# Decay masks by predicated copy, y summed by an accumulating store, the state's share of y scaled in PSUM

## The reference, cut to what matters

```python
acs = jnp.cumsum(dt * a, axis=2)                       # per chunk and head
seg = acs[:, :, :, None] - acs[:, :, None, :]
decay = jnp.exp(jnp.where(lower, seg, -jnp.inf))
cb = jnp.einsum('bctgn,bcsgn->bctsg', cc, bc)
y_diag = jnp.einsum('bctsgr,bcsgrp->bctgrp', cb[..., None] * decay, xdt)
y_off = jnp.einsum('bctgn,bcgrpn,bctgr->bctgrp', cc, s_in, jnp.exp(acs))
...
y_f, s_f = ssd_chunked(xs, dt[:, :, 0], a[0], bm, cm, h0_f)
y_b, s_b = ssd_chunked(rev(xs), rev(dt[:, :, 1]), a[1], rev(bm), rev(cm), h0_b)
y = y_f + rev(y_b) + d_skip[:, None] * xs
```

## Time and profile before

| | |
|---|---|
| runs, us | 2822.95, 2816.64, 2823.3 |
| profiled execution, us | 2829.5 |
| its span, us | 2827.7 |
| mean granted TensorE clock | 0.976 |
| TensorE matmul busy | 2672.9 us (95% of the span) |
| VectorE busy | 1658.7 us (59%) |
| ScalarE busy | 608.1 us (22%) |
| GpSimd busy | 988.0 us (35%) |

### The profile page before, as it was taken

How to read it: one execution, slowest core, us unless ns; L and a number is a source line. 1 busy time by engine, 2 the same in 40 slices (tenths; PEclk the granted TensorE clock), 3 DMA queues, 4 the chain that set the end, 5 groups by cost and what they waited for, 6 DMA issues and landing times. The chain is left out here.

```text
span 2827.7 us, 32173 instructions
## 1 busy us (share of the span) xinstructions
PE 2672.9 (95%) x12390; PEld 2146.4 (76%) x12390; DVE 1658.7 (59%) x2219; ACT 608.1 (22%) x871; POOL 988.0 (35%) x515
## 2 busy tenths in 40 slices
PE   8889999999999999987888999989989999999997
PEld 5778777778888888866775776578767888888885
DVE  6887555756556665676747986953475222222247
ACT  4222242311110011133232104632131110001111
POOL 2122225554333343541212432012645333333353
PEclk9999999999999999998999999999989999999998
DMA  3111132223222332221001343241322111111122
GB/s 139 39 51 45 51 142 82 97 82 98 97 89 91 102 96 96 97 101 61 31 30 38 112 127 112 99 177 45 116 93 90 53 45 47 50 52 45 52 69 102
DMA packets 88484, 228.88 MB, mean 81 GB/s; under 512 B 27520, under 2 KB 30720, under 8 KB 88384
## 3 DMA queue, kind: packets, MB, share of 16 engines
q1 hardware_dynamic: 52384, 172.81, 18.3%
q10 hardware_dynamic: 36000, 54.69, 6.1%
HBM read 197.98 MB, written 28.31 MB: 80 GB/s over the span
## 5 line engine op out<-in xcount | busy, mean ns | idle before, releaser
L215 POOL CAST w_hi<-w_raw 128x1024 fp32r<-128x1024 f32 x254 | 289.0, 1138 | 1774.6 <-PE ps L228 1755.8
L224 PE MATMUL ps<-a_hi,w_hi 128*128 128x512 f32 x2080 | 694.7, 402 | 47.3 <-PEq L2942 14.5
L217 POOL TENSOR_TENSOR w_lo<-w_raw,w_hi 128x1024 fp32r<-128x1024 f32 x254 | 696.0, 2740 | 20.3
L226 PE MATMUL ps<-a_lo,w_hi 128*128 128x512 f32 x2080 | 677.9, 393 | 0.0
L228 PE MATMUL ps<-a_hi,w_lo 128*128 128x512 f32 x2080 | 676.7, 393 | 0.0
L224 PEld LDWEIGHTS ps<-a_hi,w_hi 128*128 128x128 f32 x2080 | 391.4, 191 | 151.0 <-issue 58.3
L226 PEld LDWEIGHTS ps<-a_lo,w_hi 128*128 128x128 f32 x2080 | 396.1, 190 | 83.3
L228 PEld LDWEIGHTS ps<-a_hi,w_lo 128*128 128x128 f32 x2080 | 395.3, 190 | 84.3
L226 PE MATMUL ps<-g_b,w_hi 128*128 128x512 f32 x1216 | 412.6, 391 | 0.0
L224 PE MATMUL ps<-g_b,w_hi 128*128 128x512 f32 x1088 | 364.4, 392 | 11.2 <-DVE g_b L1806 11.2
L228 PE MATMUL ps<-g_b,w_lo 128*128 128x512 f32 x1088 | 362.1, 390 | 0.0
(11 more groups left out here) (459 smaller groups left out, 2682.2 us busy)
## 6 DMA issues: line engine op xcount, KB each, us to landing
w_raw<-in_wstream SPq DMA_DIRECT2D x254, 512.0 KB, 3.5
ada_w<-in_ada_w ACTq DMA_DIRECT2D x25, 512.0 KB, 3.5
ada_w_b<-in_ada_w ACTq DMA_DIRECT2D x25, 512.0 KB, 3.5
y_by_token<-y ACTq DMA_DIRECT2D x12, 512.0 KB, 3.3
x_res_b<-in_xT SPq DMA_DIRECT2D x2, 2048.0 KB, 11.2
x_block<-x_res_b SPq DMA_DIRECT2D x16, 256.0 KB, 3.0
z_rows<-ada_w ACTq DMA_DIRECT2D x8, 512.0 KB, 2.9
u_rows<-pad ACTq DMA_DIRECT2D x8, 512.0 KB, 4.2
```

The source lines that it names most:

```text
L215: pool.tensor_copy(k.w_hi[:, s, :], k.w_raw[:, s, :]).then_inc(k.w_high, 1)
L217: pool.tensor_tensor(k.w_lo[:, s, :], k.w_raw[:, s, :], k.w_hi[:, s, :].bitcast(F32), ALU.subtract).then_inc(k.w_split, 1)
L224: pe.matmul(o, w_hi, a_hi[:, c], start=first, stop=False)
L226: pe.matmul(o, w_hi, a_lo[:, c], start=False, stop=False)
```

## The change

Four things are changed, all in the scan.

1. The masks. `exponents(i, g)` is now called once for each group and writes both directions unmasked, 4 matmuls over 64 rows each: the first direction in `pair[0]`, the second in `pair[1]`. VectorE then copies the second over the first where a mask is not zero (`choose`, a predicated copy within PSUM), and ScalarE takes one exponential for each group. The 2 sums `add_decays` go. The identity matmuls and `scan_square` go.
2. The diagonal of the second direction, which the choice leaves out, is a weight for each token and head, `own`; it is computed in phase4 (products of B and C on VectorE, their sums by 16 matmuls with one column, `own_sums`) and takes the place of `d_skip` in L2656.
3. The state's share of y is scaled in place in PSUM, and the diagonal products (`own_chunk`) add onto it (`start=False`). ScalarE copies the sum out (`copy_out`).
4. y is not loaded back. GpSimd issues a store to `y_tok` that adds (`accum_op`).

The orders change with it. The diff, with declarations, sizes of waits and the loads of `stage` left out:

```diff
 # phase4, VectorE, after the fourth convolution
+            dve.wait_ge(s["silu"], 2 * XS0)
+            for g in range(NGRP):
+                for c0, c1, home in own_bc[g]:
+                    tt(home, v.bc[:, g, c0 * P:c1 * P], v.bc[:, NGRP + g, c0 * P:c1 * P], ALU.mult).then_inc(s["own_in"], 1)
 # phase4, TensorE, before the wait for sums_ready
+            for g in range(NGRP):
+                for c0, c1, home in own_bc[g]:
+                    for c in range(c0, c1):
+                        ins = pe.matmul(own_sums[:, g * NC + c:g * NC + c + 1], home[:, (c - c0) * P:(c - c0 + 1) * P],
+                                        k.mean_col[:, :], start=True, stop=True)
 # phase5, GpSimd
+            for i in range(NC):
+                pool.wait_ge(s["y_ready"], NC + i + 1)
+                pool.dma_start(d.y_tok[i, :, :], y_of[i % 2], accum_op=ALU.add).then_inc(y_out[i % 2], 16)
+            for q in range(2):
+                pool.wait_ge(y_out[q], 16 * NC // 2)
 # phase5, TensorE
+            def exponents(i, g):
                 pe.wait_ge(s["moving_ready"], i + 1)
+                if i or g:
+                    pe.wait_ge(s["e_ready"], NGRP * i + g)
+                if i and g == 0:
+                    pe.wait_ge(s["cb_ready"], i)
+                for b in range(2):
+                    at = g * HPG + b * HPG // 2
+                    for r in range(2):
+                        rows = slice(r * P // 2, (r + 1) * P // 2)
+                        ins = pe.matmul(k.ps[:, 2 * r + b, :].rearrange("p (h t) -> p h t", t=P), v.l_rows[rows, here(i)],
+                                        moving[rows, at:at + HPG // 2, :], start=True, stop=True)
             def products_cb(i):
-                pe.wait_ge(s["e_ready"], EXPS * i + 3)
+                pe.wait_ge(s["chosen"], NGRP * (i + 1))
+            def own_chunk(i, g):
+                pe.wait_ge(s["w_ready"], NGRP * i + g + 1)
+                for h in range(g * HPG, (g + 1) * HPG):
+                    ins = pe.matmul(..., start=False, stop=True)
             def forward(i):
                 ...
                 ins.then_inc(s["off_done"], 1)
+                if i + 1 < NC:
+                    exponents(i + 1, 0)
                 pe.wait_ge(s["xw_ready"], back + NC + i + 1)
                 if i:
                     pe.wait_ge(s["y_ready"], NC + i)
                 ...
                 ins.then_inc(s["st_done"], 1)
                 if i + 1 < NC:
-                    exponents(i + 1)
+                    exponents(i + 1, 1)
+                pe.wait_ge(s["fore_ready"], i + 1)
+                own_chunk(i, 0)
+                if i + 1 < NC:
                     products_cb(i + 1)
+                own_chunk(i, 1).then_inc(s["diag_done"], 1)
 # phase5, ScalarE
             def exps(i):
+                if i >= 2:
+                    act.wait_ge(s["diag_done"], i - 1)
+                for g in range(NGRP):
+                    act.wait_ge(s["chosen"], NGRP * i + g + 1)
+                    act.activation(big[:, i % 2 * NGRP + g, :], pair[0], ACT.Exp).then_inc(s["e_ready"], 1)
+            def copy_out(i):
+                act.wait_ge(s["diag_done"], i + 1)
+                if i >= 2:
+                    act.wait_ge(y_out[i % 2], 16 * (i // 2))
+                ...
+                act.activation(y_of[i % 2], Xf[(i + 1) % 2], ACT.Copy).then_inc(s["y_ready"], 1)
                 if i + 1 < NC:
                     exps(i + 1)
                     copy_cb(i + 1)
-                    if i + 2 < NC:
-                        make_moving(i + 2)
+                copy_out(i)
+                if i + 2 < NC:
+                    make_moving(i + 2)
                 if i < SPLIT_EARLY:
                     act.wait_ge(s["d_in"], 16 * (i + 1))
                     act.activation(v.a_hi[:, i, :], stage[:, :], ACT.Copy).then_inc(s["dhi"], 1)
-                act.wait_ge(s["y_ready"], NC + i + 1)
-                act.dma_start(d.y_tok[i, :, :], y_of[i % 2]).then_inc(y_out[i % 2], 16)
 # phase5, VectorE
+            def choose(i, g):
+                dve.wait_ge(s["d_done"], NGRP * i + g + 1)
+                fore, rear = (p.rearrange("p (h t) -> p h t", h=HPG) for p in pair)
+                dve.copy_predicated(fore, bc(after, 1, HPG), rear).then_inc(s["chosen"], 1)
             for i in range(NC):
-                add_decays(i)
-                if i:
-                    last_sum(i - 1)
                 dve.wait_ge(s["cb_ready"], i + 1)
                 for g in range(NGRP):
+                    dve.wait_ge(s["e_ready"], NGRP * i + g + 1)
+                    decays = big[:, i % 2 * NGRP + g, :].rearrange("p (h t) -> p h t", h=HPG)
+                    tt(decays, decays, bc(cb[:, g, :], 1, HPG), ALU.mult).then_inc(s["w_ready"], 1)
+                if i:
+                    low_part(i - 1)
                 dve.wait_ge(s["off_done"], i + 1)
+                y = heads(Xf[(i + 1) % 2])
+                tt(y, y, per_head(v.e_acs, i, 0), ALU.mult).then_inc(s["fore_ready"], 1)
+                if i + 1 < NC:
+                    choose(i + 1, 0)
                 dve.wait_ge(s["state_ready"], i + 1)
                 ch.link(tt(heads(state[:, :]), heads(state[:, :]), per_head(v.e_tot, i, 0), ALU.mult))
+                if i + 1 < NC:
+                    choose(i + 1, 1)
+                dve.wait_ge(s["st_done"], i + 1)
                 tt(state[:, :], state[:, :], Xf[i % 2], ALU.add).then_inc(s["state_ready"], 1)
                 if i + 1 < NC:
                     weigh(i + 1, 0)
```

More of the change, by code:

```diff
@@ L10 @@
 F32R = mybir.dt.float32r
+I32 = mybir.dt.int32
 ACT = mybir.ActivationFunctionType
@@ L1951, in open_scan @@
     v.rows = sb("head_rows", [P, 80])
+    v.own = sb("own_weight", [P, NC, SSM_HEADS])
     return v
@@ L2322, in _ @@
             dve.wait_ge(s["scan_in"], 16)
-            dve.tensor_copy(v.square[:, 0, :], k.mats[:, IDENT, :]).then_inc(s["chain"], 1)
-            dve.tensor_copy(v.square[:, 1:3, :], v.consts[:, 0:2 * P].rearrange("p (r t) -> p r t", r=2)).then_inc(s["chain"], 1)
+            dve.wait_ge(s["own_out"], 1)
+            for g in range(NGRP):
+                hs = slice(g * HPG, (g + 1) * HPG)
+                rear = slice(SSM_HEADS + g * HPG, SSM_HEADS + (g + 1) * HPG)
+                ch.link(tt(v.own[:, :, hs], dt[:, 0:NC, rear], bc(own_sums[:, g * NC:(g + 1) * NC], 2, HPG), ALU.mult))
+            ch.link(stt(out=v.own[:, :, :], in0=v.own[:, :, :], scalar=1.0 * D_MODEL,
+                        in1=bc(v.rows[:, 64:64 + SSM_HEADS], 1, NC), op0=ALU.mult, op1=ALU.add))
             dve.wait_ge(s["sums_rows"], 1)
@@ L2376, in phase5 @@
         BWD_JOBS = 2
-        EXPS = 2 * NGRP
-        ident_r, masks = v.square[:, 0, :], [v.square[:, 1 + r, :] for r in range(2)]
+        after = v.consts[:, SC_FORE:SC_FORE + P].bitcast(I32)
         back = 2 * CC
@@ L2453, in here @@
                 return slice(i * P, (i + 1) * P)
-            def exponents(i):
+            def exponents(i, g):
                 pe.wait_ge(s["moving_ready"], i + 1)
-                for j in range(EXPS):
-                    g, r, use = j // 2, j % 2, EXPS * i + j
-                    if use >= 2:
-                        pe.wait_ge(s["e_ready"], use - 1)
-                    if i and j == 0:
-                        pe.wait_ge(s["cb_ready"], i)
-                    rows = slice(r * P // 2, (r + 1) * P // 2)
-                    outs = [k.ps[:, 2 * r + b, :].rearrange("p (h t) -> p h t", t=P) for b in range(2)]
-                    for out in outs:
-                        pe.matmul(out, ident_r, bc(masks[r], 1, HPG // 2), start=True, stop=False)
-                    for b, out in enumerate(outs):
-                        at = g * HPG + b * HPG // 2
-                        ins = pe.matmul(out, v.l_rows[rows, here(i)], moving[rows, at:at + HPG // 2, :], start=False, stop=True)
-                    ins.then_inc(s["d_done"], 1)
+                if i or g:
[8 more added lines that the diff above has]
+                                        moving[rows, at:at + HPG // 2, :], start=True, stop=True)
+                ins.then_inc(s["d_done"], 1)
@@ L2492, in forward @@
                 if i + 1 < NC:
[L2493 removed]
+                    exponents(i + 1, 1)
+                pe.wait_ge(s["fore_ready"], i + 1)
+                own_chunk(i, 0)
+                if i + 1 < NC:
                     products_cb(i + 1)
[L2495 to L2502 removed]
+                own_chunk(i, 1).then_inc(s["diag_done"], 1)
             for q in range(2):
                 pe.wait_ge(k.pair_free[q], UZ_END // 2)
[L2506 removed]
+            for g in range(NGRP):
+                exponents(0, g)
             products_cb(0)
@@ L2513, in _ @@
             pe.wait_ge(s["dlo"], 2)
[L2514 removed]
+            pe.wait_ge(s["e_ready"], NGRP * NC)
             for e in range(2):
@@ L2655, in _ @@
                 dve.wait_ge(s["y_back"], 16 * i)
```

(2 more changed lines are left out.)

102 lines of the change are left out of this document (37 added, 65 removed).

## The result

| | before | after |
|---|---|---|
| median of 4 runs each, us | 2821.79 (2816.64 to 2823.3) | 2863.1 (2856.51 to 2866.29) |
| ratio after / before | | 1.0141, 95% 1.0122 to 1.0161 |
| profiled execution, its span, us | 2829.5, 2827.7 | 2863.94, 2862.2 |
| mean granted clock | 0.976 | 0.961 |

The change makes the kernel 1.4% slower, 41 us by the medians (34 to 45 by the interval). The forecast was 2842, within 2828 to 2862: the direction is right, the forecast change (19 us) is about half of the measured one, and the median of after lies 1 us above the upper end of that range. The medians are compared where a ratio stands; where microseconds are accounted for, the two profiled executions are, whose spans are 34.5 us apart.

The account below looks back on a forecast made before the run. VectorE's list set the pace before; afterwards a cross-engine chain through `make_moving` would bound each turn. Forward part 15.4, end of phase5 2.1 and phase4 1.8 sum to 19.3 us: 2842 predicted, range 2828 to 2862.

Parts of the forecast that it names:

- ahead of the first turn: Start of phase5's forward part: chunk 0's exponentials pass through choices, so the first `make_moving` starts about 0.6 us later.
- first turn: Forward part, first `make_moving` start to the next, without a low part: 14.70 us.
- five turns: Forward part, the turns with low parts of chunks 0 to 4: 16.70 us each.
- behind the last `make_moving`: Forward part, from chunk 7's `make_moving` start to the last diagonal product's end: 11.27 plus 9.44 us.
- forward part: Chunk loop of phase5: last diagonal product ends at 1859.5 instead of 1844.05, 15.4 us later.
- end of phase5: Copy out and accumulating store (taken at 6.5 us) behind the last products: 2.1 us later, between 0 and 6.8.
- phase4: Products of B and C delay the fifth convolution 1.1 us; the one-column sums leave 0.7: together 1.8 us.
- The clock is not in the sum: TensorE's slow stretch per turn would mostly fall beside a_hi and the low part: 0 to 1 us, up to 6.
- the ring: Cross-engine chain from one `make_moving` through choice, exponents, heads and `copy_out` to the next: 16.70 us against 13.2.
- The rival with the choice at 2.44: VectorE's predicated copy takes 2.44 us, so the last product ends 17 us later still: 2859; chance 0.14.
- the slow store: GpSimd's accumulating store takes, say, 20 us, costing 15.6 at the end of phase5: 2856; chance 0.04.
- The rival that VectorE's list would be the bound: In the chunks `make_moving` stays ahead; turns take 10.6 us against 13.2, 14 us faster overall: 2809; chance 0.12.

Follow-up runs that it names:

- e7: The changed kernel with 16 constant-data matmuls before TensorE's wait for `moving` and 6 more before the second exponents; 2857.27 us, 1.0101 to before.
- e5: e3 with 6 constant-data matmuls ahead of TensorE's wait for `moving`; 2819.55 us, 0.9974 to before.
- e3: The changed kernel with `make_moving` ahead of `copy_out` and `low_part` behind the scaling of the state; 2825.46 us, 1.0003 to before.
- e4: The changed kernel with 16 constant-data matmuls ahead of TensorE's wait for `moving` in each turn; 2865.64 us, 1.0132 to before.
- b1: The kernel before with only `make_moving` moved behind the store's wait for y; 2859.84 us, 1.0124 to before.
- e1: The changed kernel with `make_moving` moved ahead of `copy_out` on ScalarE; 2849.99 us, 1.0093 to before.
- e2: The changed kernel with `low_part` moved behind the scaling of the state on VectorE; 2836.66 us, 1.0039 to before.

## Why the prediction was right in kind and half in size

Term by term, in the profiled executions:

| term | forecast, us | measured, us |
|---|---|---|
| ahead of the first turn | 0.6 | 1.9 |
| first turn | 14.70 | 14.81 |
| five turns | 5 x 16.70 = 83.5 | 99.6 |
| behind the last `make_moving` | 20.7 | 20.76 |
| forward part, against before | +15.4 | +33.0 |
| end of phase5 | +2.1 | +1.6 |
| phase4 | +1.8 | +2.95 |
| sum | +19.3 | +37.6 |

The sum of the measured terms lies in the interval of the ratio, 34 to 45 us; the rest of the program was 3 us shorter in the profiled execution of after, which no experiment here explains and nothing in the change touches.

**The step that failed** is the last of the forecast's sum: "The clock is not in the sum ... I allow 0 to 1 us a turn, up to 6 us". With the four exponents in 0.66 us, as they are at full clock, the ring is 16.70 - 0.45 = 16.25, and five turns would be 81.3; they took 99.6, so the clock cost 18.3 us, 3.7 a turn, where 0 to 1 was allowed. In the turn of 20.55 it is in 3.47 + 0.95 + 3.56 for 1.76 + 0.55 + 1.95 (3.72) and 1.15 for 0.66 (0.49): 4.2, and 20.55 less 4.2 is 16.3. The forecast had the fall of the clock behind an idle time and the idle time of 4 us a turn, but put the slow stretch beside a_hi and the low part, where it would be covered. The rows of after put it where nothing covers it. The first exponents, right behind the idle time, still take 0.74; it is the heads and cb that run slow, and these lie on the ring. That the ring then feeds itself (pieces at half speed make the turn longer, the next exponential and `moving` come later, and TensorE idles again) fits these rows, but is argued and not shown. TensorE idles 2.25 and 1.88 us in this turn, neither as long as the 4.68 us of the earlier trace rows from which the forecast had its idea.

That the clock and not a longer ring made the turns is shown on two grounds: the sum of the rows of one turn, and e7, where turns of 16.7 and 21.3 us stand in one execution with the same list. That filling idle time raises the clock is shown by e5 against e3 (0.97 for 0.90, 4.6 us). e4 shows that filling one idle is not enough. Not shown is what made it stay at full speed in some turns of e7 and b1 and not in others.

Behind these rows: the Trainium skill (TensorE: Matmul & The Clock Gate, Part 1: The HAM clock gate) says that TensorE runs at 1.2 or 2.4 GHz, that the lower level is the default and that activity lifts it. Heads of 3.51 and 1.90 us, a ratio of 1.85, agree with two such levels. That the lower one is the default no run here shows: in the idle time from 1762 to 1765 of after the granted clock is 1.00, and it is 0.50 from 1766, when TensorE has resumed.

**What held.** The direction and its cause: `make_moving` behind a wait for the last diagonal product. b1 brings the same loss into the kernel before by that move alone; e3, which also moves the low part, takes it out of after. VectorE's list is shorter as forecast, 10.5 us a turn. The choice takes 1.23 us, where 0.69 to 3.30 was open and 1.22 was taken. The view of line L2704 in after, with the shortest, median and longest of the 16 in ns:

```profile
L2704 DVE COPY_PREDICATED ps<-scan_consts,ps x16: 1216/1229/1230, 1738.1 to 1870.0; 128x1024 f32<-128x1024 int32 x16
```

The in-place scaling takes 1.23. The rival with the choice at 2.44 is out, and so is the slow store.

**What came out right by luck.** The first turn is off by 0.1 us and the tail by 0.1, but two errors cancel in each. Each holds the four exponents twice, at 1.11 for 0.66, 0.9 us too much; and each holds about 0.9 to 1.0 us of low clock, which the forecast had at nothing. In the first turn (clock 0.79) the next state's product takes 3.02 us and holds the second exponents up by 0.4 to 0.5, and these take 1.22 for 0.73; in the tail (clock 0.89) the first exponents take 1.22 and the product 2.96. With the start of the part (below) the clock cost some 21 us in the forward part. It is luck, too, that the time came out near the upper end of the range: that end was made of a choice of 2.44 us with some microseconds of clock, and the choice took 1.23.

**What was mis-sized, with little effect.** The four exponents: 0.73 us and not 1.18. The two halves of the rows run beside each other, as the rule that the forecast quotes from the Trainium skill (TensorEngine Tiling (Array Packing), Key Properties) had it. This overstates a turn with a low part by 0.45 us, and the start, the first turn and the tail by 0.9 each. The start, 1.9 us late for 0.6: the table load of the exponential (1.28 us) ran from 1733.71 to 1734.99 before, 0.26 us past the end of the first exponents; after, it comes behind the wait for the choice (1739.43 to 1740.71), and all of it is on the path. The clock, 0.50 there from 1742, adds 0.9 (second exponents 1.17 for 0.73, cb 1.22 for 0.71); against both stands the 0.9 by which the exponents were counted too high. Phase4: the fifth convolution is 0.9 us late, near the 1.1 forecast, and the one-column products cost 0.4 for 0.7; what was left out is again the clock behind a longer idle, 1.6 us. The accumulating store: 5.3 us for 6.5, and the end 1.6 for 2.1.

**The rival that VectorE's list would be the bound** (2809) is what only both orders together come near: e3's turns are 11.6 to 12.6 us, for the 10.6 of the rival. The place of `make_moving` is half of it; the rival took a_hi and the low part's wait out together with `make_moving`, and e1 shows that these close a second ring. It also took 13.2 for every turn of before, where they are 13.2 and 13.8 by turns.

## What to carry to other kernels

Where an edit moves an instruction behind a wait, draw the ring that it closes and sum it at both clock levels: the matmuls on it at the durations that rows show for full speed and for half; if TensorE idles in the turn, the sum at half speed belongs in the range; here it did with idle times of 2 us. The instructions saved on VectorE were worth nothing here until the order on its neighbour was redone: two moves turned +1.4% into no change, and a few constant matmuls in the largest gap and one step of phase4 moved made that -0.3%. Price the wait in front of a one-time instruction as well (a table load behind a wait is no longer hidden).

## What the runs showed of the hardware

- Four 64-row matmuls of 512 columns, two in each half of the rows, take 0.73 us as a group; a pair in one half alone took as long. The Trainium skill (TensorEngine Tiling (Array Packing), Key Properties) says that different tiles execute in parallel; the trace agrees.
- A predicated copy of 128x1024 float32 within PSUM, with its mask in SBUF, takes 1.23 us of VectorE, as a copy out of PSUM does.
- A store of 512 KB issued by GpSimd lands after 2.9 us, with accumulation after 5.2 to 5.4; its issue takes GpSimd 0.53 to 0.70 us, with accumulation 0.86 to 1.02. The Trainium skill (DMA: Bandwidth & Descriptors, Anatomy of one DMA — SWDGE (gpsimd) path) gives 3.2 us for this size: near the plain store, 2 us short for the accumulating one.
- The granted clock fell to 0.50 in a list with idle times of 1.88 and 2.25 us in a turn of 20.55, and was there for 88 of 147 us. The length of one idle time does not decide: in e3 a turn with a longest idle time of 1.63 us had 1.00 throughout, the next, with 1.64, had 0.86; in e2, in the turn shown, 4.00 us slowed only the pieces right behind it. In the kernel before, with TensorE busy 12.15 of 13 us, it never fell in this part.
